# First step of the up stage split ahead of its border, first rows of the output stage split ahead of theirs, last stores waited for later

## The reference, cut to what matters

```
def _merge_and_norm(x, oa, ga, ob, gb, oc, gc, gates, w_br, w_o, ln_g, ln_b):
    B, S = x.shape[:2]
    br = jnp.stack([oa.reshape(B, S, BR_W) * jax.nn.silu(ga),
                    ob.reshape(B, S, BR_W) * jax.nn.silu(gb),
                    oc.reshape(B, S, BR_W) * jax.nn.silu(gc)], axis=2)
    up = jnp.einsum('bsnw,nwd->bsnd', br, w_br)
    mixed = (jax.nn.sigmoid(gates.reshape(B, S, 3, D_MODEL)) * up).sum(axis=2)
    y = jnp.einsum('bsd,de->bse', mixed, w_o)
    return _layernorm(ALPHA * x + y, ln_g, ln_b)
```

## Time and profile before

| | us |
|---|---|
| median of 3 runs (3206.63 to 3220.13) | 3210.12 |
| profiled execution, its own time | 3213.99 |
| its span, first to last instruction | 3211.9 |
| TensorE busy in it | 3029.9 |
| VectorE busy | 1443.6 |
| ScalarE busy | 858.3 |
| GpSimd busy | 522.6 |

### The profile page before, as it was taken

How to read it: one execution, slowest core, us unless ns; L and a number is a source line. 1 busy time by engine, 2 the same in 40 slices (tenths; PEclk the granted TensorE clock), 3 DMA queues, 4 the chain that set the end, 5 groups by cost and what they waited for, 6 DMA issues and landing times. The chain is left out here.

```text
span 3211.9 us, 48659 instructions
## 1 busy us (share of the span) xinstructions
PE 3029.9 (94%) x18900; PEld 2616.9 (81%) x18900; DVE 1443.6 (45%) x3317; ACT 858.3 (27%) x1945; POOL 522.6 (16%) x494
## 2 busy tenths in 40 slices
PE   5999998999999999898989999989999999998988
PEld 4788887888888886698878888878888888867987
DVE  6214233445555443365632142444455544334556
ACT  3221222333323332211121112233342233322110
POOL 0000000344344410000000000004433544000000
PEclk9999998999999999999999999989999999998999
DMA  5432215434443338664443322154424532494633
GB/s 196 147 103 86 92 52 165 144 94 122 116 124 101 112 93 282 212 207 155 163 149 129 96 86 80 50 190 121 132 80 125 140 110 83 108 352 148 223 128 118
DMA packets 344997, 434.45 MB, mean 135 GB/s; under 512 B 60740, under 2 KB 248516, under 8 KB 344572
## 3 DMA queue, kind: packets, MB, share of 16 engines
q1 hardware_dynamic: 330180, 405.99, 40.7%
q10 hardware_dynamic: 14592, 25.37, 2.3%
HBM read 302.78 MB, written 131.27 MB: 135 GB/s over the span
## 5 line engine op out<-in xcount | busy, mean ns | idle before, releaser
L456 PE MATMUL proj_acc<-proj_wh,keep_xh 128*128 128x512 f32 (+1 forms) x1152 | 451.5, 392 | 13.9 <-DVE keep_xl L576 13.5
L458 PE MATMUL proj_acc<-proj_wh,keep_xl 128*128 128x512 f32 (+1 forms) x1152 | 445.5, 387 | 0.0
L457 PE MATMUL proj_acc<-proj_wl,keep_xh 128*128 128x512 f32 (+1 forms) x1152 | 444.8, 386 | 0.0
L1597 ACT ACTIVATE att_p<-att_ss,att_stat 128x257 f32<-128x257 f32 (+9 forms) x384 | 249.4, 650 | 620.0 <-DVE att_stat L1646 608.7
L1653 DVE COPY att_pt<-att_tr 128x256 f32<-128x256 f32 (+3 forms) x384 | 176.6, 460 | 524.1 <-PE att_tr L1540 523.6
L1646 DVE TENSOR_REDUCE att_stat<-att_ss 128x1 f32<-128x257 f32 (+9 forms) x384 | 245.1, 638 | 54.1 <-PE att_ss L1526 30.9
L456 PEld LDWEIGHTS proj_acc<-proj_wh,keep_xh 128*128 128x128 f32 x1152 | 217.2, 189 | 57.0 <-DVE keep_xl L576 17.6
L458 PEld LDWEIGHTS proj_acc<-proj_wh,keep_xl 128*128 128x128 f32 x1152 | 217.2, 189 | 41.0
L457 PEld LDWEIGHTS proj_acc<-proj_wl,keep_xh 128*128 128x128 f32 x1152 | 217.6, 189 | 38.1
L1540 PE MATMUL att_tr<-keep_ident,att_p 128*128 128x128 f32 x1392 | 227.1, 281 | 0.5 <-ACT att_pt L1604 0.5
L2418 PE MATMUL up_acc<-up_bh,up_wh 128*128 128x384 f32 x576 | 195.1, 339 | 25.6 <-DVE up_wl L2475 25.6
(11 more groups left out here) (347 smaller groups left out, 5986.0 us busy)
## 6 DMA issues: line engine op xcount, KB each, us to landing
keep_hold<-in_w_in SPq DMA_DIRECT2D x56, 512.0 KB, 4.0
up_gates<-scratch_gatesT SPq DMA_DIRECT2D x18, 1536.0 KB, 7.6
scratch_gatesT<-att_gout SPq DMA_DIRECT2D x140, 192.0 KB, 1.9
keep_early<-in_w_in SPq DMA_DIRECT2D x40, 512.0 KB, 3.6
str_va<-in_cache_a_v SPq DMA_DIRECT2D x16, 1024.0 KB, 9.0
str_ka<-in_cache_a_kT SPq DMA_DIRECT2D x14, 1024.0 KB, 11.2
scratch_sg<-proj_out SPq DMA_DIRECT2D x54, 256.0 KB, 2.0
scratch_brt<-att_o SPq DMA_DIRECT2D x48, 256.0 KB, 2.2
```

The costliest lines, as they stand in the source:

```text
L456: nc.tensor.matmul(bank, hi, mh, start=kt == 0, stop=False)
L457: nc.tensor.matmul(bank, hi, ml, start=False, stop=False)
L458: mm = nc.tensor.matmul(bank, lo, mh, start=False, stop=kt == KT - 1)
L1597: nc.scalar.activation(p[:, s, place], ss[:, s, place], ACT.Exp, bias=stat[:, m % 4, 0:1], accum_out=stat[:, m % 4, 1:2]).then_inc(exp_rea ...
```

## The change

In the stream stage SP also loads block 0 of the up stage (`b0`, behind the loads of n = 2); ScalarE and VectorE split it, and the first three weight pieces, at the stage's end, into tiles that live across the border. SP no longer waits there for br2's store: its semaphore lives on and is waited for ahead of the up stage's block 6. In the up stage the loads of block 0 and its splits are gone, the weight pieces run six steps ahead of the step (three of them already made), and in its last block the rows of output tile 0 and the first half row of W_o are split into the tiles that held the three weight pieces. The stores of the last span get a semaphore of their own, which the output stage waits for ahead of loading tile 6. The output stage splits W_o in half rows, all of the first half's first, and starts with what is split already. The weights' tiles are laid out by piece instead of by row.

The diff, cut to its core:

```diff
+LEAD = 3
+
+
+def first_weight(C, d):
+
+    return C["early"][:].rearrange("p k d -> p (k d)").rearrange("p (k c) -> p k c", k=BR // P)[:, :, P * d:P * (d + 1)]
...
+                if n == 2:
+                    src = S["brt"].rearrange("(n k p) t -> n p k t", k=BR // P, p=P)[0]
+                    sp.dma_start(C["b0"][:], src[:, :, 0:FSPAN]).then_inc(b0_loaded, 16)
...
-            sp.dma_start(S["br2"][own], res[:]).then_inc(stored, 16)
-            sp.wait_ge(early_loaded, 48)
-            sp.wait_ge(stored, 16 * (2 * H + 1))
+            sp.dma_start(S["br2"][own], res[:]).then_inc(C["res_stored"], 16)
+            sp.wait_ge(stored, 16 * 2 * H)
...
             take(taken + 1, ptc[:].rearrange("p j n -> p (j n)"))
+            act.wait_ge(b0_loaded, 16)
+            for of, hi, _ in b0_halves:
+                nc.scalar.activation(hi, of, ACT.Copy).then_inc(b0_hi, 1)
+            act.wait_ge(early_loaded, 48)
+            for d in range(LEAD):
+                nc.scalar.activation(C["w0h"][:, d], first_weight(C, d), ACT.Copy).then_inc(w0_hi, 1)
...
             out_b(NB - 1)
+            for g, (of, hi, lo) in enumerate(b0_halves):
+                dve.wait_ge(b0_hi, g + 1)
+                nc.vector.tensor_tensor(lo, of, hi.bitcast(F32), ALU.subtract)
             out_c(NB - 1)
+            for d in range(LEAD):
+                dve.wait_ge(w0_hi, d + 1)
+                nc.vector.tensor_tensor(C["w0l"][:, d], first_weight(C, d), C["w0h"][:, d].bitcast(F32), ALU.subtract)
...
-    wh, wl = ph.sb("wh", [P, 3 * KN, D], F32R), ph.sb("wl", [P, 3 * KN, D], F32R)
-    braw = ph.sb("braw", [P, 2, KN, W])
-    bh, bl = ph.sb("bh", [P, 2, KN, W], F32R), ph.sb("bl", [P, 2, KN, W], F32R)
+    wh, wl = ph.sb("wh", [P, 3 * KT - LEAD, KN, P], F32R), ph.sb("wl", [P, 3 * KT - LEAD, KN, P], F32R)
+    braw = (C["b0"], ph.sb("b1", [P, KN, W]))
+    bh, bl = (C["bh0"], ph.sb("bh1", [P, KN, W], F32R)), (C["bl0"], ph.sb("bl1", [P, KN, W], F32R))
     gates = ph.sb("gates", [P, 2, KT, W])
-    mix = ph.sb("mix", [P, 2, KT, W])
+    mix = C["mix"]
+    (o_hi, o_first_hi), (o_lo, o_first_lo) = first_output(C)
+    mh0_made, wo_hi = ph.sem("mh0_made"), ph.sem("wo_hi")
...
+    def weight_halves(n, d):
+
+        i = KT * n + d
+        return (C["w0h"][:, i], C["w0l"][:, i]) if i < LEAD else (wh[:, i - LEAD], wl[:, i - LEAD])
...
-                if j >= 2:
-                    sp.wait_ge(bl_made, 2 * (j - 1))
+                if j >= 3:
+                    sp.wait_ge(bl_made, 2 * (j - 2))
...
+                if n == 0:
+                    sp.wait_ge(C["res_stored"], 16)
...
-            load_b(0)
             load_gates(0)
             load_b(1)
...
-            sp.wait_ge(wl_made, 6)
+            sp.wait_ge(wl_made, 6 - LEAD)
...
-                    sp.wait_ge(wl_made, 3 * KT)
+                    sp.wait_ge(wl_made, 3 * KT - LEAD)
...
-            sp.wait_ge(early_loaded, 48)
...
-                pe.wait_ge(bl_made, 2 * (j + 1))
+                if j:
+                    pe.wait_ge(bl_made, 2 * j)
...
-                    if s == 0:
-                        pe.wait_ge(wl_made, KT * n + d + 1)
+                    if s == 0 and i >= LEAD:
+                        pe.wait_ge(wl_made, i - LEAD + 1)
...
-            for g in range(2):
-                high(0, g)
-            for i in range(LEAD):
+                nc.scalar.activation(weight_halves(n, d)[0], raw_weights(n, d), ACT.Copy).then_inc(wh_made, 1)
+
+            for i in range(LEAD, 2 * LEAD):
                 weights(i)
             for j, (s, n) in enumerate(FS):
                 for d in range(KT):
-                    i = KT * j + d + LEAD
+                    i = KT * j + d + 2 * LEAD
...
-                                      mix[:, s % 2, d - 3:d + 1, :]).then_inc(stored[s % 2], 16)
-            act.wait_ge(stored[0], 64)
+                                      mix[:, s % 2, d - 3:d + 1, :]).then_inc(stored[s % 2] if s < 2 else C["mix_stored"], 16)
+                    if (s, n, d) == (2, 2, 1):
+                        act.wait_ge(early_loaded, 48)
+                        act.wait_ge(up_made, KT * (j - 1))
+                        for g in range(2):
+                            nc.scalar.activation(o_hi[:, 4 * g:4 * g + 4, :], first_mix(C)[:, 4 * g:4 * g + 4, :], ACT.Copy,
+                                                 scale=0.5).then_inc(mh0_made, 1)
+                    if (s, n, d) == (2, 2, 4):
+                        nc.scalar.activation(o_first_hi, early_tile(C, 0)[:, 0:512], ACT.Copy).then_inc(wo_hi, 1)
             act.wait_ge(stored[1], 32)
...
+                    if (s, n, d) in ((2, 2, 2), (2, 2, 3)):
+                        g = d - 2
+                        dve.wait_ge(mh0_made, g + 1)
+                        at = slice(4 * g, 4 * g + 4)
+                        nc.vector.scalar_tensor_tensor(out=o_lo[:, at, :], in0=first_mix(C)[:, at, :], scalar=0.5,
+                                                       in1=o_hi[:, at, :].bitcast(F32), op0=ALU.mult, op1=ALU.subtract)
+                    if (s, n, d) == (2, 2, 4):
+                        dve.wait_ge(wo_hi, 1)
+                        nc.vector.tensor_tensor(o_first_lo, early_tile(C, 0)[:, 0:512], o_first_hi.bitcast(F32), ALU.subtract)
...
+def first_mix(C):
+
+    return C["early2"][:, EARLY_O - EARLIEST, :].rearrange("p (k c) -> p k c", k=KT)
+
+
+def first_output(C):
+
+    flat = [C[name][:].rearrange("p d k c -> p (d k c)") for name in ("w0h", "w0l")]
+    return [(tile[:, 0:KT * P].rearrange("p (k c) -> p k c", k=KT), tile[:, KT * P:KT * P + 512]) for tile in flat]
...
+    SPLITS_O = [(half, k) for half in range(2) for k in range(KT)][1:]
+    (o_hi, o_first_hi), (o_lo, o_first_lo) = first_output(C)
+
+    def weight_halves(half, k):
+
+        if half == 0 and k == 0:
+            return o_first_hi, o_first_lo
+        return [w[:, k, 512 * half:512 * half + 512] for w in (wh, wl)]
+
+    def mix_halves(t):
+
+        return (mh[:, t % 2], ml[:, t % 2]) if t else (o_hi, o_lo)
...
-                    sp.wait_ge(ml_made, 2 * (t - 1))
+                    sp.wait_ge(ml_made, 2 * (t - 2))
+                if t == 6:
+                    sp.wait_ge(C["mix_stored"], 32)
...
-                    sp.wait_ge(wl_made, EARLY_O)
-                    sp.wait_ge(ml_made, 2)
+                    sp.wait_ge(wl_made, KT - 1 + EARLY_O)
...
-                pe.wait_ge(ml_made, 2 * (t + 1))
+                if t:
+                    pe.wait_ge(ml_made, 2 * t)
+                high, low = mix_halves(t)
                 for half in range(2):
                     a = 2 * u + half
                     if t >= 2:
                         pe.wait_ge(y_taken, 2 * (t - 2) + half + 1)
-                    cols = slice(512 * half, 512 * half + 512)
                     for k in range(KT):
-                        if t == 0 and half == 0:
-                            pe.wait_ge(wl_made, k + 1)
-                        nc.tensor.matmul(acc[:, a, :], mh[:, u, k, :], wh[:, k, cols], start=k == 0, stop=False)
-                        nc.tensor.matmul(acc[:, a, :], mh[:, u, k, :], wl[:, k, cols], start=False, stop=False)
-                        mm = nc.tensor.matmul(acc[:, a, :], ml[:, u, k, :], wh[:, k, cols], start=False, stop=k == KT - 1)
+                        if t == 0 and (half, k) in SPLITS_O:
+                            pe.wait_ge(wl_made, SPLITS_O.index((half, k)) + 1)
+                        hi, lo = weight_halves(half, k)
+                        nc.tensor.matmul(acc[:, a, :], high[:, k, :], hi, start=k == 0, stop=False)
+                        nc.tensor.matmul(acc[:, a, :], high[:, k, :], lo, start=False, stop=False)
+                        mm = nc.tensor.matmul(acc[:, a, :], low[:, k, :], hi, start=False, stop=k == KT - 1)
...
-            high(0)
-            for k in range(KT):
-                if k == EARLY_O:
+            for half, k in SPLITS_O:
+                if (half, k) == (0, EARLY_O):
                     act.wait_ge(raw_loaded, 16 * (KT - EARLY_O))
-                nc.scalar.activation(wh[:, k, :], raw_tile(k), ACT.Copy).then_inc(wh_made, 1)
+                nc.scalar.activation(weight_halves(half, k)[0], raw_tile(k)[:, 512 * half:512 * half + 512], ACT.Copy)\
+                    .then_inc(wh_made, 1)
...
-            low(0)
-            for k in range(KT):
-                dve.wait_ge(wh_made, k + 1)
-                nc.vector.tensor_tensor(wl[:, k, :], raw_tile(k), wh[:, k, :].bitcast(F32), ALU.subtract)\
+            for i, (half, k) in enumerate(SPLITS_O):
+                hi, lo = weight_halves(half, k)
+                dve.wait_ge(wh_made, i + 1)
+                nc.vector.tensor_tensor(lo, raw_tile(k)[:, 512 * half:512 * half + 512], hi.bitcast(F32), ALU.subtract)\
...
+            KN = BR // P
+            with nc.sbuf_tensor(f"keep_res{l}", [P, BR], F32) as res, nc.sbuf_tensor(f"keep_b0{l}", [P, KN, FSPAN], F32) as b0, \
```

(35 more changed lines are left out.)

36 lines of the change are left out of this document (16 added, 20 removed).

## The result

After: 3193.63 us (median of 4 runs, 3189.24 to 3196.23), against 3213.1 for before (4 runs, 3206.63 to 3220.13). The ratio is 0.9929, 95% interval 0.991 to 0.9947: faster by 0.7%, some 19 to 23 us. The forecast was 28 us less, 3182, with 3173 to 3197 as its range. The profiled execution took 3193.43 us (span 3191.6, mean granted clock 0.978), 20.6 less than the one before.

The account below looks back on a forecast made before the run. TensorE was taken to bound the kernel, its waits being what can be won. 22.95 us at stream to up plus 2 x 2.5 at up to output made 28, so a median of 3182 us, range 3173 to 3197.

Parts of the forecast that it names:

- Border A's waits: Stream to up stage: TensorE starts up earlier, by 9.80 us in layer 0 and 10.87 in layer 1.
- the br2 wait: End of stream stage: SP no longer waits for br2's store, which lands 2.0 us after issue; 1.66 per border.
- The br1 stores: End of stream stage: expected down before br2's issue; the forecast counts as wrong if br0 or br1 stores end last.
- Covers ahead of border A: Stream stage's end: new ScalarE copies (4.0 us at most) and VectorE subtractions fit into idle time, cost 0.
- the gates behind it: Up stage's start: gates land about 6.3 us after issue, before TensorE needs VectorE; cost 0.
- The load in the stream queue: Stream stage: 768 KB takes 2.1 us against ka's slack of 2.06; cost 0, bounds 0 and 2.1 per layer.
- Border B: Up to output stage: earlier start less half-clock cost gains 2.5 us per layer, bounds 1.0 and 4.2.
- The wait for W_o rows: Output stage's first half tile: TensorE stands 4.4 us until W_o rows 5 to 7 are loaded and split.
- The clock at border A: Stream to up stage: clock holds over the 2.45 us pause, gaining 2.28 us in layer 0, 0 in layer 1.
- the second: Clock falls at stream-to-up border and W_o rows come late: 2.28 and 3.0 us less gain, 3187; chance 0.15.
- The third: At all four borders another store or engine ends last: 4 x 1.66 and 2.28 lost, 9 us, 3191; chance 0.12.
- The fourth: Stream stage: new load delays ka beyond its slack; delay d costs d - 2.06 per layer, slower at d = 24; chance 0.03.

Follow-up runs that it names:

- e5: After, with the two waits for last stores (br2, last mixT) put back where they were; 3198.39 us, ratio 0.9943 to before.
- e4: After, with nine extra transposes into a free bank at three TensorE waits near the stream stage's end; 3185.26 us, ratio 0.9895 to before.
- e1: After, with up's end and the output stage of before, so only the stream-to-up border is changed; 3199.89 us, ratio 0.9942 to before.
- e8: The kernel of e7 with the nine transposes of e4 and twelve more behind the stream's last product; 3171.33 us, ratio 0.9861 to before.
- e3: After, with the first five W_o rows multiplied for both halves of the first output tile before rows 5 to 7; 3193.75 us, ratio 0.9915 to before.
- e6: After, with the 768 KB load in the stream queue made three times; 3208.12 us, ratio 0.9969 to before.
- e10: After, unchanged, measured once more beside its own before; 3188.68 us, ratio 0.9916 to before.
- e9: Before, with only nine extra transposes at three TensorE waits near the stream stage's end; 3207.98 us, ratio 0.9976 to before.
- e7: The row order of e3, plus second tile split ahead of first tile's addition and norm weights waited for only at the norm; 3179.59 us, ratio 0.9894 to before.

## Why the prediction came out as it did

- **Border A's waits: right.** 9.62 and 10.70 us of idle time gone (forecast 9.80 and 10.87); the barrier cost 1.41 (1.29), and e5 puts the br2 wait at 1.70 (1.66). The br1 stores, which the forecast named as a sign of being wrong, didn't end last in after, but they did in layer 1 of e4 and of e1.
- **Covers ahead of border A, and the gates behind it: right.** VectorE went on with the gates at 1349.51, 6.8 us behind their issue (forecast 6.3), and TensorE waited for none. In after TensorE ran at the half clock there; e8, which ran at the full one, waited for none either.
- **The load in the stream queue: 0 in after's profile, but not a safe 0.** There is no wait on ka in after. With the same one load e3, e4 and e8 waited once each, and lost 0.4 to 2.35 us in that layer; the bound of 2.1 had about the size. e6 shows that the next 4.2 us of transfers cost 8.6 us of waiting and 17.8 us of time over both layers, so what the forecast's row lacked was the clock that falls with such a wait. The Trainium skill, DMA: Bandwidth & Descriptors, section Specifications, sets a limit of about 358 GB/s for a core's HBM traffic; by that rule two more loads take an estimated 4.4 us, and the waits of 3.92 and 4.68 agree. The trace itself stands 3% above that limit, at 368 GB/s over 20 us.
- **Border B: right in sum, and partly for another reason.** Forecast 2.5 per layer, measured 3.0 and 2.6. The wait for W_o rows came as forecast (4.45 us for 4.4), and the clock fell behind it. But the gain hangs on the earlier first transfer: without it the splits gave 0.1 (e5). A split made ahead of a border whose next operand is not there was worth next to nothing here.
- **The clock at border A: wrong.** The step that failed is "the new idle time is 2.45 us, shorter than those 3.7, so the clock should hold". One fall 3.7 us after a last matmul was taken for a rule. After's profile doesn't test it, since the clock was low from 1327 on, but its sign failed: the first 16 matmuls ran at 0.50, not 1.00. In the five layers that came to the border at full clock (e1, e4 twice, e6, e10) the clock fell, in three of them with a pause of 2.63. The term's size was right, 2.28: where the clock does hold (e8) the up stage is 2.3 to 2.4 us shorter per layer.
- **A term that was not in the sum.** The forecast took layer 0's stream end from a trace in which it ran at full clock, and added the change to that. Of 18 such ends 4 did. After's profile had it at 1.2 GHz: 5.6 us more in layer 0. The forecast saw this pair (3.79 and 7.09) in layer 1, gave it bounds of 3.3 there and none in layer 0; over the whole tail the two layers of before differ by 5.75 (14.94 and 9.19). With 2.28 and 5.6 taken off, 28 becomes 20.1; the profiles stand 20.3 apart. That it fits so closely is in part luck: the terms that are left miss by 0.35, 0.45 and 0.6 us, and these nearly cancel.

Of the rivals, the second (clock lost at border A, W_o late) came true in the price of its first half and in 1.2 of its 3.0 us: W_o's rows were met 7.50 and 7.63 us behind the first transfer, 7.13 and 6.81 in before. The third did not, and e5 shows what its waits would have cost: 1.70 at border A, but 3.2 at border B, where the 1.66 was too small by the forecast's own rows (1505.13 to 1509.22 is 4.09, less 1.29 makes 2.8). The fourth did not in after. e6 agrees with its formula for the wait (a delay of 6.4 less 2.06 is 4.3), and shows that the time lost is up to 12.0 per layer.

The measured 3193.63 lies in the range, near its upper end. That end was made of rival 3 and of 2.1 us per layer lost in the stream (by these terms it is 3195, not 3197), and neither came about in after's profile. The loss at the stream's end stood in no bound for layer 0, so that the range held is in part luck.

The second measure of after (e10) came out 27 us under its before, the first 19 to 23. The scatter goes with this clock: e9, whose stream ends held it in its profile, spread over 3205 to 3210 in 10 runs, at a granted clock of 0.978 to 0.979, and before beside it over 3211 to 3221 in 16, at 0.972 to 0.977. The Trainium skill, TensorE: Matmul & The Clock Gate, Part 1 (The HAM clock gate), says that the monitor runs freely and does not start over with a kernel, so that one kernel meets it at different phases; 4 ends of 18, in e10's two layers one of each, are what that would look like. That it is the phase which decides here was not tried by itself.

## What to carry to other kernels

Price the engine's clock as a stage has it over several executions or layers, not as the one trace at hand has it; two layers of one trace that differ are the warning. A few microseconds of short pauses, or one barrier, can cost more in clock than in waiting, and idle matmuls into a free bank, behind nothing that anybody waits for, are a cheap cover. A load that takes up the whole slack of a full queue will be waited for in some executions, and a wait of half a microsecond cost the clock as well. Where a stage waits for a load that can only start behind its border, move the border's opening or the work that needs no load, and then look at the next engine's queue: a wait for something that is needed much later held up the split that was needed now.

## What the runs showed of the hardware

- TensorE fell to 1.2 GHz at the end of the stream stage after pauses of 0.67 and 0.55 us in a stretch in which it was otherwise busy (1.33 and 1.45 us of the two windows of 2 us ahead), in 14 of 18 cases, and never in 6 in which those pauses were filled.
- At border A it fell about 1.4 us behind the last matmul in e10's layer 0, and with matmuls running again in e4's layer 0 (0.77 in the microsecond from 1339). In a pause of 2.59 us at border B it held in after and fell in e7's layer 0 (0.61 in the microsecond from 1501).
- A wait of 0.58 us for a load was followed by the half clock in e4's layer 1, and cost 2.25 us; waits of 3.92 and 4.68 in e6 cost 5.8 and 12.0.
- The mixT store that is no longer waited for runs beside the W_o loads: ScalarE met them 7.50 and 7.63 us after the first was issued, against 7.13 and 6.81 in before and 7.19 and 6.94 in e5, where the store is waited for. The overlap that the forecast bounded at 1.5 us cost 0.3 to 0.8.
